# Where levels 2 to 5 of the prompt's recurrence stand on TensorE, and in which PSUM banks

## The reference, cut to what matters

```python
def step(S, inp):
    qi, bi, ki, vi = inp
    diff = bi[:, :, :, None, :] - bi[:, :, None, :, :]
    decay = jnp.exp(jnp.where(causal[:, :, None], diff, NEG_BIG))
    att = jnp.einsum('bhtc,bhsc,bhtsc->bhts', qi, ki, decay)
    o = jnp.einsum('bhts,bhsv->bhtv', att, vi) + jnp.einsum('bhtc,bhcv->bhtv', qi * jnp.exp(bi), S)
```

## Time and profile before

| what | value |
|---|---|
| median of 3 runs | 804.24 us (803.9 to 804.75) |
| the profiled execution | 804.06 us, its span 802.3 us |
| TensorE (PE) busy | 794.0 us, 99% of the span |
| DVE, ACT, POOL busy | 71%, 55%, 34% |
| granted TensorE clock, mean | 0.998 |
| chain that ended last | PE 98%, DVE 1%, DMA 1% |

### The profile page before, as it was taken

How to read it: one execution, slowest core, us unless ns; L and a number is a source line. 1 busy time by engine, 2 the same in 40 slices (tenths; PEclk the granted TensorE clock), 3 DMA queues, 4 the chain that set the end, 5 groups by cost and what they waited for, 6 DMA issues and landing times.

```text
span 802.3 us, 17681 instructions
## 1 busy us (share of the span) xinstructions
PE 794.0 (99%) x6786; PEld 781.8 (97%) x6786; DVE 567.8 (71%) x774; ACT 437.9 (55%) x629; POOL 274.4 (34%) x246
## 2 busy tenths in 40 slices
PE   9999999999999999999999999999999999999996
PEld 8999999999999999999999999999999999999996
DVE  7978798577877666554587788966798676645552
ACT  6665567554666665344354646665455666644442
POOL 3599393056700000122149817702663000001220
PEclk9999999999999999999999999999999999999999
DMA  8797879968567588767558968997766677787751
GB/s 315 225 338 286 308 235 311 264 225 301 185 210 258 192 292 288 253 239 250 193 174 226 370 256 282 266 269 247 269 228 205 222 234 255 239 285 249 249 209 54
DMA packets 126035, 199.75 MB, mean 249 GB/s; under 512 B 19642, under 2 KB 115690, under 8 KB 118506
## 3 DMA queue, kind: packets, MB, share of 16 engines
q1 hardware_dynamic: 124682, 196.48, 73.8%
q10 hardware_dynamic: 1296, 2.48, 0.8%
HBM read 191.03 MB, written 51.90 MB: 303 GB/s over the span
## 4 chain that ended last, share of the span: by engine, by line
PE 98%; DVE 1%; DMA 1%; ACT 0%; DVEq 0%; issue 0%; ACTq 0%
PE main L663 88%; PE small L663 4%; PE small L749 1%; PE small L720 1%; DMA raw<-in_w_in 1%; PE small L944 0%; PE small L736 0%; DVE h_lo L1331 0%; PE small L759 0%; PE small L767 0%; PE small L801 0%; DVE x L1711 0%; DVE w_lo_rows L1321 0%; PE small L903 0%; PE small L870 0%; PE small L712 0%
## 5 line engine op out<-in xcount | busy, mean ns | idle before, releaser
L1059 ACT ACTIVATE w_hi_rows<-raw 128x1024 fp32r<-128x1024 f32 (+1 forms) x256 | 266.5, 1042 | 228.8 <-PE main L663 141.9
L1315 DVE TENSOR_TENSOR w_lo_rows<-raw,w_hi_rows 128x1024 fp32r<-128x1024 f32 (+1 forms) x256 | 338.9, 1324 | 64.7 <-ACT w_hi_rows L1059 63.2
L663 PE MATMUL main<-h_hi,w_hi_rows 128*128 128x264 f32 x1312 | 373.9, 287 | 0.2 <-DVE h_lo L1331 0.2
L663 PE MATMUL main<-h_lo,w_hi_rows 128*128 128x264 f32 x1312 | 369.0, 283 | 0.0
L663 PE MATMUL main<-h_hi,w_lo_rows 128*128 128x264 f32 x1312 | 362.7, 283 | 0.2 <-DVE w_lo_rows L1321 0.2
L663 PEld LDWEIGHTS main<-h_hi,w_hi_rows 128*128 128x128 f32 x1312 | 246.8, 188 | 3.8 <-issue 2.5
L663 PEld LDWEIGHTS main<-h_lo,w_hi_rows 128*128 128x128 f32 x1312 | 246.8, 188 | 0.0
L663 PEld LDWEIGHTS main<-h_hi,w_lo_rows 128*128 128x128 f32 x1312 | 243.0, 188 | 0.4 <-DVE w_lo_rows L1321 0.4
L663 PE MATMUL main<-a_hi,w_hi_rows 128*128 128x264 f32 x512 | 145.4, 284 | 0.0
L663 PE MATMUL main<-a_lo,w_hi_rows 128*128 128x264 f32 x512 | 144.9, 283 | 0.0
L663 PE MATMUL main<-a_hi,w_lo_rows 128*128 128x264 f32 x512 | 144.9, 283 | 0.0
(11 more groups left out here) (241 smaller groups left out, 960.7 us busy)
## 6 DMA issues: line engine op xcount, KB each, us to landing
raw<-in_w_in SPq DMA_DIRECT2D x48, 1024.0 KB, 5.9
raw<-in_w_up SPq DMA_DIRECT2D x32, 1024.0 KB, 5.3
raw<-in_w_down SPq DMA_DIRECT2D x32, 1024.0 KB, 5.2
out_kvs<-in_cache SPq DMA_DIRECT2D x48, 512.0 KB
out_kvs<-in_cache SPq DMA_DIRECT2D x32, 496.0 KB
raw<-in_w_o SPq DMA_DIRECT2D x8, 1024.0 KB, 5.8
raw<-in_w_br SPq DMA_DIRECT2D x8, 768.0 KB, 5.7
gates<-q_scratch SPq DMA_DIRECT2D x4, 768.0 KB, 7.7
```

Source lines behind the costliest of these rows:

```text
L663: return pe.matmul(out[:, TOK - 1::-1], w, rhs[:, ::-1], start=start, stop=stop)
L1059: act.activation(w_hi[:, slot(l, u), 0:k, :], raw_of(u, k), ACT.Copy).then_inc(w_hi_ready, 1)
L1315: dve.tensor_tensor(w_lo[:, slot(l, u), 0:k, :], raw_of(u, k), w_hi[:, slot(l, u), 0:k, :].bitcast(F32), ALU.subtract).then_inc(w_lo_ready, 1)
```

## The change

Levels 2, 3, 4 and 5 all run after unit 12, on TensorE and in DVE's masking alike; nothing is put in after unit 10 any more. Levels 2 and 3 share a turn of two banks (2 in columns 0 to 255, 3 in columns 256 to 511), and so do levels 4 and 5. The bank is signalled ready after the odd level's matmuls, and signalled taken after the odd level's masks. POOL's waits before levels 6 to 8 and before the final keys go by the shared banks, so before level 6 it waits until levels 2 and 3 are both done on TensorE. `TURNS` is four turns shorter, and every later name keeps its bank.

```diff
--- before.py
+++ after.py
@@ -79,14 +79,15 @@
 L_COLS = FOLD_AT[8]
 LV_SLOTS = 4
 VALUE_PARTS = range(0, 4), range(4, 6)
-LEVELS_AT = ((10, (2, 3)), (12, (4, 5)), (14, (6,)), (17, (7, 8)))
+LEVELS_AT = ((12, (2, 3, 4, 5)), (14, (6,)), (17, (7, 8)))
+SHARED = range(2, 6)
 
 
 TURNS = (
     ["norm1"]
     + ["sample values T"]
     + [f"first levels {hp} {h}" for hp in range(2) for h in range(2)]
-    + [f"level {i} {h}" for i in range(2, 7) for h in range(2)]
+    + [f"level {i} {h}" for i in (2, 4, 6) for h in range(2)]
     + ["values T"] + [f"level {i} {h}" for i in range(7, 9) for h in range(2)]
     + ["decayed keys T", "sample rows T", "recurrence", "scores 0 0", "scores 1 0"]
     + ["scores 0 1", "scores 1 1", "sample states"]
@@ -355,6 +356,18 @@
         waits_over = sem("waits_over")
 
 
+        def level_bank(i, h):
+
+            return f"level {i - i % 2 if i in SHARED else i} {h}"
+
+        def level_columns(i):
+
+            return i % 2 * PROMPT if i in SHARED else 0
+
+        def last_of_bank(i):
+
+            return i not in SHARED or i % 2 == 1
+
         def use_bank(pe, l, name):
 
             i = TURN[name]
@@ -741,15 +754,16 @@
             def level(l, i):
 
                 pe.wait_ge(level_ready, l * 8 + i)
-                banks = [use_bank(pe, l, f"level {i} {h}") for h in range(2)]
+                banks = [use_bank(pe, l, level_bank(i, h)) for h in range(2)]
+                first = level_columns(i)
                 for hp in range(2):
                     late = queries_of(i)[:, hp, :].rearrange("p (n s t) -> p n s t", s=2, t=LEVELS[i - 1])[:, :, 1, :]
                     for h in range(2):
                         rows = slice(h * HD, (h + 1) * HD)
-                        mm = pe.matmul(banks[h][:, hp * P:hp * P + P], k_lv[rows, i % LV_SLOTS, hp, :], late[rows],
+                        mm = pe.matmul(banks[h][:, first + hp * P:first + hp * P + P], k_lv[rows, i % LV_SLOTS, hp, :], late[rows],
                                        start=True, stop=True)
-                        if hp == 1:
-                            done(mm, f"level {i} {h}")
+                        if hp == 1 and last_of_bank(i):
+                            done(mm, level_bank(i, h))
 
             def scores(l, part):
 
@@ -1427,14 +1441,15 @@
                     mask = levels[:, FOLD_AT[i]:FOLD_AT[i] + 4 * n].rearrange("p (a n) -> p a n", a=4)
                     mask = mask.unsqueeze(3).to_broadcast([P, 4, n, half])
                     for h in range(2):
-                        bank = take(dve, l, f"level {i} {h}")
+                        bank = take(dve, l, level_bank(i, h))
                         wait_ends(dve)
                         dst = att[:, h, :, :].rearrange("p a (n s t) -> p a n s t", s=2, t=half)[:, :, :, 1, :]
-                        src = bank[:, 0:4 * HALF].rearrange("p (a n t) -> p a n t", a=4, n=n)
+                        src = bank[:, level_columns(i):level_columns(i) + 4 * HALF].rearrange("p (a n t) -> p a n t", a=4, n=n)
                         dve.copy_predicated(dst, mask.bitcast(U32), src).then_inc(masked, 1)
                     for h in range(2):
                         dve.wait_ge(masked, l * 20 + 8 + 2 * (i - 2) + h + 1)
-                        dve.sem_inc(bank_taken[TURN[f"level {i} {h}"] % 4], 1)
+                        if last_of_bank(i):
+                            dve.sem_inc(bank_taken[TURN[level_bank(i, h)] % 4], 1)
 
                 def mask_scores(part):
 
@@ -1757,7 +1772,7 @@
                 z_ready(pool, l, CT_CQ + 1)
                 for i, half in enumerate(LEVELS, 1):
                     if i >= 2 + LV_SLOTS:
-                        take(pool, l, f"level {i - LV_SLOTS} 1")
+                        take(pool, l, level_bank(i - LV_SLOTS, 1))
                     def halves(t, s, half=half):
 
                         return t.rearrange("p h (n s t) -> p h n s t", s=2, t=half)[:, :, :, s, :]
@@ -1790,7 +1805,7 @@
                         step(pool.tensor_tensor(cum[:, :, 1, :], cum[:, :, 1, :],
                                                 cum[:, :, 0, half - 1:half].to_broadcast([P, n, half]), ALU.mult))
 
-                take(pool, l, "level 5 1")
+                take(pool, l, level_bank(5, 1))
                 for tb in range(2):
                     own = slice(tb * P, tb * P + P)
                     ins = pool.tensor_tensor(q_lv[:, 1, :, own][:, :, ::1 - 2 * tb], kg[:, :, own], suf_f[:, :, own],
```

## The result

The changed kernel takes 807.03 us (median of 6 runs, 806.76 to 807.91), against 804.09 us (6 runs) before: ratio 1.0036, 95% interval 1.0026 to 1.0046. It is 2.9 us slower. I had forecast 804.8 with a range of 803.2 to 806.2, so the time lies outside. The profiled execution took 807.02 us, its span 805.2.

What follows compares the result with a forecast made beforehand. PE, busy 99% of the span, was taken to bound the kernel. First layer -0.39 + 1.4, second -0.39, together +0.6 us: 804.7 against the profiled execution, 804.8 for the median, range 803.2 to 806.2.

Steps and rivals of the forecast that it cites:

- What the visit costs: PE, both layers: one visit to the levels fewer saves 0.39 us a layer, 0.78 us in all.
- Level 5's keys: First layer, merged visit: POOL's keys come at 51.5 us, PE wants them at 50.1 and waits 1.4 us.
- collisions at cum_f and at the keys: First layer: DVE's low parts lengthen POOL's L1790 from 0.68 to 1.52 us and delay level 5's keys to 51.44.
- POOL held before level 6 in the second layer: Second layer: POOL waits 3.3 us, until 442.2, for the bank of levels 2 and 3.
- costs nothing: Second layer's POOL wait of 3.3 us and DVE's eight masks in a row: no added wait of PE.
- POOL's own idle time of 5.78 us: Second layer, POOL before L1820: this idle time takes up the 3.3 us delay.
- no bank wait is added on PE: Merged visit and level 6: the banks they need are masked in time, so PE waits 0 us more.
- Rival B: Second layer's rotary operations: late POOL catches four DVE instructions, costing PE 2.0 us; +2.6 in all, 806.8; chance 0.07.
- L1814's catch: Second layer: POOL's L1814 lengthened DVE's L1541 to 3.58 us; this catch of 1.9 us was to go away.
- A slip in the signs: Expected profile, second layer: 48 matmuls of 0.1203 us to each side of the merged visit behind unit 12.

Runs made afterwards that it cites:

- the version where nothing takes its place: Changed kernel with levels 2 to 4 behind unit 12, 5 and 6 behind unit 14, level 7's masks before the low part: 803.31 us, ratio 0.9988.
- merging alone: The kernel before with levels 2 to 5 behind unit 12, each level in banks of its own: 811.78 us, ratio 1.0090.

## Why the prediction was wrong

- **What the visit costs: right.** 0.39 us a layer forecast, 0.40 in the second layer's chain, and 0.9 us in the version where nothing takes its place.
- **Level 5's keys: right in kind, a little large.** Forecast were collisions at cum_f and at the keys and 1.4 us of waiting; the rows show both collisions, and PE loses 1.26 us (0.88 of it shown as idle time). This execution ran 0.2 us ahead there and the keys were ready at 51.0, not 51.4.
- **POOL held before level 6 in the second layer: right** in size (3.58 against 3.3), **wrong in "costs nothing"**. I followed it to POOL's own idle time of 5.78 us and stopped: that time took up the delay for what POOL delivers, but not for whom POOL meets on the way. In the first layer I kept POOL where it was and asked for its collisions only up to level 5.
- **The step that failed is "no bank wait is added on PE".** I checked the banks of the merged visit and of level 6, and no later turn. "decayed keys T" takes level 7's bank; its masks are the last thing of DVE's longest stretch. PE's list of waits was empty there before, and I took that for slack. The rows of the masks and of the transposes in both layers, 0.65 and 1.02 us apart, would have shown that the first layer had less room than the second. There, any lengthening of the rotary stretch counts in full.
- **Rival B had the place and not the mechanism.** It named the rotary stretch of the second layer and POOL's delay, but priced them by the low part of unit 19 (slack 0.8 us) and gave it 0.07. It also held that L1814's catch "goes away, as that instruction moves behind unit 17": it moved onto unit 17's rotary sum. And it took the first layer as evidence that nothing happens there; the first layer lost more (1.59 us) than the second (0.83). That its 806.8 lies near the measured 807.0 is luck: it has no loss in the first layer and a larger one in the second.
- **Size.** Forecast +0.6: -0.78 and +1.4. Measured +2.9: -0.8, +1.26 and +2.42, the last not in my sum.
- **A slip in the signs.** I wrote of 48 matmuls to each side of the merged visit; by the change there are 96 ahead of it, units 9 to 12, as the chain shows.

## What to carry to other kernels

An engine that shows no wait at a place may have no slack there either: before moving work, compare the start of the consumer with its supplier's, in each layer, for every semaphore that it waits on downstream, bank turns included, not just at the place of the change. Where two engines keep each other out, shifting one of them in time is a change to both, and its price lies where the next long instruction of one meets the other's tight stretch. Merging visits to a busy engine pays only as far as the suppliers and the consumers of the merged work still have room on both sides; here, with level 7's masks first in both, splitting DVE's masks 6 and 4 rather than 8 and 2 (with level 5 at its later place) was worth 1.6 us, twice what the merge saves.

## What the runs showed of the hardware

The granted clock fell to 0.50 behind a visit with 1.91 and 0.31 us of idle time (merging alone, both layers) and stayed at 1.00 behind single waits of 0.88 and 1.35 us (the change), in the same stream: 2.2 us of idle time cost 1.6 more afterwards. A DVE subtraction of two SBUF operands of 128 x 1024 takes 1.21 us alone and 2.96 us when POOL's 128 x 1024 product stands before it, which itself took 3.29 instead of 1.94. A consumer can stand on its supplier's limit with no wait shown: the transposes stood 0.65 us behind the masks with none, and 0.64 behind them with one of 1.35 us. A visit to small matmuls in the middle of the fp32r stream costs some 0.4 us beside its matmuls (16 records: 1.31 us of which 0.92 are the records), and a boundary between two groups inside a visit costs nothing that shows (32 records in one visit: 2.00 us, against 1.10 for 16).
